# Combination of the experts' rows: two rows of a token sorted by place, the front ones gathered and added during the last expert, no stage of its own

## The chip, the core and the metric

The kernel runs on one core of a Trainium2 chip. The metric is the device time of one launch in microseconds (us), lower is better; the kernel before is shown with the median of three launches. The engines of the core are TensorE (PE in the profile), VectorE (DVE), ScalarE (ACT), GpSimd (POOL) and SyncE (SP, which here only issues transfers), beside 16 DMA engines.

## What is computed

A decoder block over 1,024 tokens of width 1,024: a mixer (linear recurrence and attention side by side), a residual addition, then a mixture of 32 experts, a residual addition and a last RMSNorm. The change is in the last part. Of the reference:

```python
e_in_group = jnp.take_along_axis(e_logits, g_sel[:, :, None], axis=1)[:, 0]
top_v, top_i = lax.top_k(e_in_group, TOP_K)             # TOP_K = 2
comb_w = p_group * jax.nn.softmax(top_v, axis=-1)
expert = g_sel * EXPERTS_PER_GROUP + top_i
...
    hb = jax.nn.silu(xb @ w1[e]) * (xb @ w3[e])
    return hb @ w2[e]
...
out = jnp.zeros((T + 1, D), xn.dtype).at[slot_tok].add(y * slot_w[:, None])[:T]
...
x = x + hierarchical_moe(v, ...)
return rms_norm(x, g_final)
```

Each token goes to two different experts of one group; the output is the residual plus the two experts' rows, each times its weight, and then normed.

## The kernel before

The program is a list of stages (`write`); at the end of each, `stage` clears the semaphores and puts an all-engine barrier. The last two stages are `experts` and `combine`.

**`experts`.** The tokens of an expert fill up to 96 slots (`BLK`); expert j owns the slots 96j to 96j+95 of the DRAM tensor `y_d`. What is over 96 goes to surplus blocks behind slot 96*32; their number n is known only on the chip, and `beyond` runs them under a condition. For each expert, SP loads six 1 MB pieces of weights into a ring of 12 buffers (`e_raw`), ACT makes the high part of each (`piece_hi`), DVE the low part (`piece_lo`, L1505), and PE runs three products for each pair. POOL gathers the tokens of expert j+2 by an indirect transfer (L1575). At the end ACT copies the 96 result rows out of PSUM (`rows_out`, L1649) and issues their store to `y_d` (`rows_store`, L1653), which signals `y_stored[j % 2]`. The experts go through `body(j, b)`, with the copy and the store of expert j-1 inside the pass of expert j. Each engine has its own instruction order, written out by hand; between the first passes DVE also works out the slots of the tokens in small steps (`surplus`, `places`, `destinations`, `blocks`), the slot of a token's first and second choice going to `dest`.

**`combine`.** After the barrier, with eight tiles of 128 tokens: POOL gathers for tile t the two rows of each token from `y_d` (two indirect transfers of 512 KB, L1913) into a ring of four pairs of buffers; DVE adds both, each times its weight, to the residual `x2` (L1956, one operation SCALAR_TENSOR_TENSOR of 128x1024 a row); ACT squares and sums (L1935); DVE makes the mean (L1942); POOL takes its power -0.5 (L1908, `root`); DVE scales by it and by `g_final` (L1949, `norm`); SP stores the tile (L1927). DVE's order is: both additions of t, mean of t-1, norm of t-2.

## Time and profile before

| | |
|---|---|
| three launches | 1899.32, 1899.99, 1902.91 us (median 1899.99) |
| profiled execution | 1900.84 us, span from first to last instruction 1899.2 us |
| busy: PE, DVE, ACT, POOL | 91%, 56%, 45%, 7% of the span |
| matmul share after 1852 us (`combine`) | none |

A row of a timeline is: start in us, duration in us, engine, line of the kernel, operation, output<-input, shapes, count, and in brackets how long the engine had been idle and what ended that. "ACTq" and "SPq" are transfers issued by these engines. A transfer issued by POOL (DMA_INDIRECT) shows the time in which POOL made it ready, not its landing. A row of windows is: the stretch, its length, busy time of each engine with the number of instructions, granted TensorE clock, busy share of the DMA engines, GB/s.

### The profile page before, as it was taken

How to read it: one execution, taken by the hardware profiler on the slowest of the kernel's cores; microseconds unless marked ns; L12 is line 12 of the kernel's file. 1: busy time of each engine (PE TensorE's matmuls, PEld its weight loads, DVE VectorE, ACT ScalarE, POOL GpSimd, SP SyncE). 2: the span in 40 equal slices, each digit the busy share in tenths (PEclk: the TensorE clock that was granted, in tenths of full speed). 3: DMA queues.
4: the chain of work that ended last, by engine and by line, in shares of the span. 5: the costliest groups of instructions: out<-in, count | busy, mean ns of one | idle time of the engine just before them, and what ended most of it. 6: DMA issues, size and time to landing. Idle time of an engine off the chain costs nothing. (4 is left out here: it accounts for less than half of the span.)

```text
span 1899.2 us, 22922 instructions
## 1 busy us (share of the span) xinstructions
PE 1727.1 (91%) x8515; PEld 1375.4 (72%) x8515; DVE 1061.3 (56%) x1211; ACT 849.1 (45%) x861; POOL 131.1 (7%) x179
## 2 busy tenths in 40 slices
PE   4999999999999998988887989959999999999970
PEld 3788888888986887866675879846677777777750
DVE  4343434341215103257775342669988888888856
ACT  5233424241211212135554020237777777777751
POOL 1200000000000000011110000010000000000005
PEclk9999999999999999989998989979999999999995
DMA  5722312223431233534434250179999999999947
GB/s 173 210 89 72 115 66 99 88 88 109 146 122 45 90 113 122 196 133 178 177 121 155 89 181 12 66 251 398 393 399 395 394 400 392 393 397 397 397 193 276
DMA packets 147070, 386.02 MB, mean 203 GB/s; under 512 B 11448, under 2 KB 70920, under 8 KB 142928
## 3 DMA queue, kind: packets, MB, share of 16 engines
q1 hardware_dynamic: 133760, 338.97, 48.0%
q0 software_dynamic: 8384, 29.63, 5.3%
q10 hardware_dynamic: 4880, 16.82, 2.2%
q8 instruction: 28, 0.46, 0.1%
q14 instruction: 18, 0.15, 0.0%
HBM read 317.96 MB, written 67.42 MB: 203 GB/s over the span
## 5 line engine op out<-in xcount | busy, mean ns | idle before, releaser
L1505 DVE TENSOR_TENSOR e_l<-e_raw,e_h 128x2048 fp32r<-128x2048 f32 x192 | 439.4, 2291 | 67.1 <-ACT e_h L1499 66.9
L1499 ACT ACTIVATE e_h<-e_raw 128x2048 fp32r<-128x2048 f32 x192 | 368.0, 1918 | 84.8 <-PE ps L1534 50.1
L196 PE MATMUL ps<-uh,w_h 128*128 128x512 f32 x1024 | 318.2, 392 | 21.2 <-DVE ul L838 13.5
L196 PE MATMUL ps<-ul,w_h 128*128 128x512 f32 x1024 | 317.1, 391 | 0.0
L196 PE MATMUL ps<-uh,w_l 128*128 128x512 f32 x1024 | 316.9, 391 | 0.0
L180 DVE TENSOR_TENSOR w_l<-w_raw,w_h 128x2048 fp32r<-128x2048 f32 x38 | 87.1, 2291 | 349.6 <-ACT w_h L176 349.6
L196 PEld LDWEIGHTS ps<-uh,w_h 128*128 128x128 f32 x1024 | 193.1, 189 | 63.1 <-issue 22.3
L196 PEld LDWEIGHTS ps<-ul,w_h 128*128 128x128 f32 x1024 | 193.5, 189 | 40.5
L196 PEld LDWEIGHTS ps<-uh,w_l 128*128 128x128 f32 x1024 | 193.4, 189 | 40.5
L1521 PE MATMUL ps<-e_h,e_xth 128*96 128x512 f32 x512 | 205.1, 401 | 5.8 <-DVE e_l L1505 2.7
L1521 PE MATMUL ps<-e_h,e_xtl 128*96 128x512 f32 x512 | 202.6, 396 | 0.0
L1521 PE MATMUL ps<-e_l,e_xth 128*96 128x512 f32 x512 | 201.8, 394 | 0.0
L176 ACT ACTIVATE w_h<-w_raw 128x2048 fp32r<-128x2048 f32 x38 | 72.7, 1914 | 228.7 <-DMA w_raw<-w_in 104.5
L208 PE MATMUL ps<-w_h,uh 128*128 128x256 f32 x384 | 112.3, 293 | 10.6 <-DVE ul L1341 5.8
L1521 PEld LDWEIGHTS ps<-e_h,e_xth 128*96 128x96 f32 x512 | 83.0, 162 | 45.7 <-issue 7.2
L208 PE MATMUL ps<-w_l,uh 128*128 128x256 f32 x384 | 110.8, 288 | 0.0
L208 PE MATMUL ps<-w_h,ul 128*128 128x256 f32 x384 | 110.7, 288 | 0.0
L1521 PEld LDWEIGHTS ps<-e_h,e_xtl 128*96 128x96 f32 x512 | 83.0, 162 | 36.2
L1521 PEld LDWEIGHTS ps<-e_l,e_xth 128*96 128x96 f32 x512 | 83.3, 163 | 32.0
L208 PEld LDWEIGHTS ps<-w_h,uh 128*128 128x128 f32 x384 | 75.8, 197 | 13.5 <-issue 6.2
L1534 PE MATMUL ps<-e_h,e_hth 128*96 128x512 f32 x256 | 82.2, 402 | 2.1 <-DVE e_htl L1644 2.1
L987 PE MATMUL ps<-at_qk 128*128 128x512 f32 (+3 forms) x288 | 74.5, 392 | 9.5 <-DVE at_small L1077 6.8
(254 smaller groups left out, 2256.5 us busy)
## 6 DMA issues: line engine op xcount, KB each, us to landing
e_raw<-w_exp_gate SPq DMA_DIRECT2D x64, 1024.0 KB, 20.9
e_raw<-w_exp_up SPq DMA_DIRECT2D x64, 1024.0 KB, 20.8
e_raw<-w_exp_down SPq DMA_DIRECT2D x64, 1024.0 KB, 19.8
w_raw<-w_in SPq DMA_DIRECT2D x28, 1024.0 KB, 5.5
qk_d<-qk SPq DMA_DIRECT2D x16, 1024.0 KB, 4.1
at_qk<-qk_d SPq DMA_DIRECT2D x8, 2048.0 KB, 8.7
y_d<-e_y ACTq DMA_DIRECT2D x32, 384.0 KB, 6.4
y_d<-zeros POOLq DMA_DIRECT2D x22, 384.0 KB, 10.8
```

Of the source, the lines that this page charges most:

```text
L176: act.activation(self.w_h[s][:, :, :], self.w_raw[s][:, :, :], ACT.Copy).then_inc(self.w_hi[s], 1)
L180: dve.tensor_tensor(self.w_l[s][:, :, :], self.w_raw[s][:, :, :], self.w_h[s][:, :, :].bitcast(F32), ALU.subtract).then_inc(self.w_lo[s], 1)
L196: mm = pe.matmul(ps[:, h * HALF:(h + 1) * HALF], w[:, k, :], u[:, k, h * HALF:(h + 1) * HALF], start=first, stop=last)
L208: mm = pe.matmul(ps, u[:, k, rows], w[s][:, k, :], start=first, stop=last)
L987: mm = pe.matmul(k_.ps[n % 2][:, at:end], q, qk[c][:, part, at:end], start=first, stop=last)
L1499: act.activation(self.e_h[m % SPLIT][:, :, :], self.e_raw[slot][:, :, :], ACT.Copy).then_inc(self.e_hi[m % SPLIT], 1)
L1505: dve.tensor_tensor(self.e_l[slot][:, :, :], self.e_raw[slot][:, :, :], self.e_h[m % SPLIT][:, :, :].bitcast(F32), ALU.subtract).then_inc( ...
L1521: mm = pe.matmul(ps, x[:, k, :], w[:, k, :], start=first and first_piece, stop=last and last_piece)
L1534: mm = pe.matmul(ps[:, c * HALF:(c + 1) * HALF], x[:, at, :], w[:, 2 * k + c, :], start=first, stop=last)
```

## The change

`combine` and the barrier ahead of it go away. DVE, in two more places between the first experts, sorts the two slots of each token into the lower (`EARLY`) and the higher (`LATER`), and their weights with them (`row_order`, `shares`). When expert 30's rows are stored, POOL gathers all lower rows into eight buffers `near` and DVE adds them after its last work on expert 31. When all rows are stored, POOL gathers the higher rows into eight buffers `far`; then come addition, squares, mean, power, norm and store as before, the norm writing into `far[t]`. The lower row of a token may lie in a surplus block; then a third gather runs (`SURPLUS`), only if n > 0. `near` and `far` lie over the weights' buffers. `g_final` is loaded behind the last weights. The power -0.5 of the tiles comes on POOL behind all eight `LATER` gathers, where it stood between the gathers before. The core of the diff:

```diff
+        tok = self.tok = high.put("rt_tok", [P, NT], I32)
+        self.rows_of = high.put("rows_of", [P, 3, NT], I32)
+        self.share = high.put("share", [P, 3, NT])
+        self.final_at = high.at
...
+        order = Map(nc, self.list_end + 16 * NE, self.high)
+        dst = [order.put(f"ls_dst{s}", [P, NT]) for s in range(2)]
+        swapped, kept, here, one, two, row = (order.put(f"ls_{n}", [P, NT]) for n in ("swapped", "kept", "here", "one", "two", "row"))
+        final = Map(nc, self.final_at, self.high)
+        g_b = final.put("cb_g", [P, D])
+        total, mean, rstd, power = (final.put(f"cb_{n}", [P, NT]) for n in ("total", "mean", "rstd", "power"))
+        upper = Map(nc, self.act_start, self.raw_end)
+        near, far = ([upper.put(f"cb_{n}{t}", [P, D]) for t in range(NT)] for n in ("near", "far"))
+        EARLY, LATER, SURPLUS = range(3)
...
-        def beyond(engine, body):
+        def beyond(engine, body, before=None, after=None):
 
             engine.wait_ge(listed_out, 1)
             n = engine.value_load(k_.blocks[0:1, n_over:n_over + 1], min_val=0, max_val=MAXX)
             with engine.If(0 < n):
+                if before:
+                    before()
                 with engine.Fori(0, MAXX // 2) as i:
                     for b in range(2):
                         with engine.If(2 * i + b < n):
                             body(NE + 2 * i + b, b, 2 * i + b)
+                if after:
+                    after(n)
             return n
...
-                beyond(sp, other)
+                sp.dma_start(g_b[:, :], k_.ins["g_final"].partition_broadcast(P)).then_inc(g_in, 16)
+                beyond(sp, other, before=lambda: sp.wait_ge(near_added, NT))
+                for t in range(NT):
+                    sp.wait_ge(normed, t + 1)
+                    sp.dma_start(k_.out[t * P:(t + 1) * P, :], far[t][:, :]).then_inc(out_stored, 16)
+                sp.wait_ge(out_stored, 16 * NT)
...
+                pool.memset(power[:, :], -0.5).then_inc(const, 1)
+
+                def rows(which, t, to, done):
+                    upto = BLK * (NE - 1) if which == EARLY else SLOTS
+                    pool.indirect_dma_start(out=to[t][:, :], out_offset=None, in_=k_.y_d[0:upto, :],
+                                            in_offset=bass.IndirectOffsetOnAxis(ap=k_.rows_of[:, which, t:t + 1], axis=0))\
+                        .then_inc(done[t], 16)
+
+                def all_stored(n):
+                    pool.wait_ge(y_stored[0], 16 * (NE // 2 + (n + 1) // 2))
+                    pool.wait_ge(y_stored[1], 16 * (NE // 2 + n // 2))
+
+                def surplus_rows(n):
+                    pool.wait_ge(const, 1)
+                    pool.wait_ge(near_added, NT)
+                    all_stored(n)
+                    pool.tensor_tensor(mean[:, :], power[:, :], power[:, :], ALU.mult).then_inc(surplus_ready, 1)
+                    pool.wait_ge(surplus_ready, 1)
+                    for t in range(NT):
+                        rows(SURPLUS, t, near, near_in)
+
+                pool.wait_ge(ordered, 3)
+                pool.wait_ge(y_stored[0], 16 * (NE // 2))
+                pool.wait_ge(y_stored[1], 16 * (NE // 2 - 1))
+                for t in range(NT):
+                    rows(EARLY, t, near, near_in)
+                n = beyond(pool, lambda j, b, t: gather(pool, j, b, None, t), after=surplus_rows)
+
+                all_stored(n)
                 pool.wait_ge(idx_in[0], 16 * (n // 2 + 1))
                 pool.wait_ge(idx_in[1], 16 * ((n + 1) // 2))
+                pool.wait_ge(const, 1)
+                pool.tensor_tensor(rstd[:, :], power[:, :], power[:, :], ALU.mult).then_inc(const, 1)
+                pool.wait_ge(const, 2)
+                for t in range(NT):
+                    rows(LATER, t, far, far_in)
+                for t in range(NT):
+                    pool.wait_ge(averaged, t + 1)
+                    pool.tensor_tensor(rstd[:, t:t + 1], mean[:, t:t + 1], power[:, t:t + 1], ALU.pow).then_inc(powered, 1)
...
+                for t in range(NT):
+                    act.wait_ge(added, t + 1)
+                    act.activation(near[t][:, :], k_.x2[:, t, :], ACT.Square, accum_out=total[:, t:t + 1]).then_inc(squared, 1)
...
+                LAST = BLK * (NE - 1)
+
+                def row_order():
+                    tt(swapped[:, :], dst[0][:, :], dst[1][:, :], ALU.is_gt)
+                    tt(kept[:, :], dst[0][:, :], dst[1][:, :], ALU.is_le)
+                    tt(row[:, :], dst[0][:, :], dst[1][:, :], ALU.max)
+                    dve.tensor_copy(k_.rows_of[:, LATER, :], row[:, :]).then_inc(ordered, 1)
+                    tt(dst[0][:, :], dst[0][:, :], dst[1][:, :], ALU.min)
+                    did(dve.tensor_scalar(here[:, :], dst[0][:, :], float(LAST), None, ALU.is_lt))
+                    did(dve.tensor_scalar(dst[1][:, :], dst[0][:, :], float(LAST - 1), None, ALU.min))
+                    dve.tensor_copy(k_.rows_of[:, EARLY, :], dst[1][:, :]).then_inc(ordered, 1)
+                    did(dve.tensor_scalar(dst[0][:, :], dst[0][:, :], float(LAST), None, ALU.max))
+                    dve.tensor_copy(k_.rows_of[:, SURPLUS, :], dst[0][:, :]).then_inc(ordered, 1)
+
+                def shares():
+                    for which, of_kept, of_swapped in ((LATER, 1, 0), (EARLY, 0, 1)):
+                        tt(one[:, :], kept[:, :], k_.wgt[:, of_kept, :], ALU.mult)
+                        tt(two[:, :], swapped[:, :], k_.wgt[:, of_swapped, :], ALU.mult)
+                        tt(k_.share[:, which, :], one[:, :], two[:, :], ALU.add)
+                    tt(one[:, :], k_.share[:, EARLY, :], here[:, :], ALU.mult)
+                    tt(k_.share[:, SURPLUS, :], k_.share[:, EARLY, :], one[:, :], ALU.subtract)
+                    did(dve.tensor_copy(k_.share[:, EARLY, :], one[:, :]))
+
+                def add(rows, which, t, done):
+                    dve.scalar_tensor_tensor(out=k_.x2[:, t, :], in0=rows[t][:, :], scalar=k_.share[:, which, t:t + 1],
+                                             in1=k_.x2[:, t, :], op0=ALU.mult, op1=ALU.add).then_inc(done, 1)
+
+                def surplus_rows(n):
+                    dve.wait_ge(near_added, NT)
+                    for t in range(NT):
+                        dve.wait_ge(near_in[t], 32)
+                        add(near, SURPLUS, t, surplus_added)
+                    dve.wait_ge(surplus_added, NT)
+
+                def average(t):
+                    dve.wait_ge(squared, t + 1)
+                    dve.tensor_scalar(mean[:, t:t + 1], total[:, t:t + 1], 1.0 / D, EPS, ALU.mult, ALU.add).then_inc(averaged, 1)
+
+                def norm(t):
+                    dve.wait_ge(powered, t + 1)
+                    dve.scalar_tensor_tensor(out=far[t][:, :], in0=k_.x2[:, t, :], scalar=rstd[:, t:t + 1],
+                                             in1=g_b[:, :], op0=ALU.mult, op1=ALU.mult).then_inc(normed, 1)
...
+                body(4, 0)
+                row_order()
+                body(5, 1)
+                shares()
+                in_pairs(dve, body, 3, NE // 2 - 1)
                 body(NE - 2, 0, True)
                 j, b = NE - 1, 1
                 k_.piece_lo(dve, (j, b, 4))
                 hidden(dve, j, (j, b, 3))
                 k_.piece_lo(dve, (j, b, 5))
                 h_low(dve, j)
+                for t in range(NT):
+                    dve.wait_ge(near_in[t], 16)
+                    add(near, EARLY, t, near_added)
...
-                beyond(dve, other)
-
-    def combine(self):
...
+                beyond(dve, other, after=surplus_rows)
                 dve.wait_ge(g_in, 16)
                 for t in range(NT):
...
+                    dve.wait_ge(near_added, t + 1)
+                    dve.wait_ge(far_in[t], 16)
+                    add(far, LATER, t, added)
                     if t >= 1:
-                        averages(t - 1)
+                        average(t - 1)
                     if t >= 2:
                         norm(t - 2)
-                averages(NT - 1)
+                average(NT - 1)
                 for t in (NT - 2, NT - 1):
                     norm(t)
...
-                             (self.experts,), (self.combine,)):
+                             (self.experts,)):
```

How the instructions stand on the engines, at three places. POOL at the end, before: `cb_y` are the buffers of the ring, one row a gather.

```order
L1579 DMA e_idx_5175<-slots_d 96x1
L1664 TENSOR_LOAD blocks
...
L1903 MEMSET cb_power 128x8
L1913 DMA cb_y_8525<-y_d,dest 128x1024
L1913 DMA cb_y_8526<-y_d,dest 128x1024
...
L1913 DMA cb_y_8532<-y_d,dest 128x1024
L1908 TENSOR_TENSOR cb_rstd<-cb_mean,cb_power 128x1
```

And in the changed kernel: `near` for the lower rows, `far` for the higher.

```order
L1593 DMA e_idx_5175<-slots_d 96x1
L1738 MEMSET cb_power 128x8
L1742 DMA cb_near_6655<-y_d,rows_of 128x1024
...
L1742 DMA cb_near_6662<-y_d,rows_of 128x1024
L1678 TENSOR_LOAD blocks
...
L1770 TENSOR_TENSOR cb_rstd<-cb_power 128x8
L1742 DMA cb_far_6663<-y_d,rows_of 128x1024
...
L1742 DMA cb_far_6670<-y_d,rows_of 128x1024
L1776 TENSOR_TENSOR cb_rstd<-cb_mean,cb_power 128x1 x8
```

Eight of the sixteen gathers now stand ahead of the read of n, and all powers stand behind the last gather.

DVE between expert 4 and the next weights, in the changed kernel; before, row L1505 stood right behind the row of `e_xtl`.

```order
L1637 TENSOR_TENSOR e_xtl_6632<-ps,e_xth_6630 128x768
L1870 TENSOR_TENSOR ls_swapped<-ls_dst_6642,ls_dst_6643 128x8
L1870 TENSOR_TENSOR ls_kept<-ls_dst_6642,ls_dst_6643 128x8
L1870 TENSOR_TENSOR ls_row<-ls_dst_6642,ls_dst_6643 128x8
L1908 CAST rows_of<-ls_row 128x8
L1870 TENSOR_TENSOR ls_dst_6642<-ls_dst_6642,ls_dst_6643 128x8
L1910 TENSOR_SCALAR ls_here<-ls_dst_6642 128x8
L1911 TENSOR_SCALAR ls_dst_6643<-ls_dst_6642 128x8
L1912 CAST rows_of<-ls_dst_6643 128x8
L1913 TENSOR_SCALAR ls_dst_6642<-ls_dst_6642 128x8
L1914 CAST rows_of<-ls_dst_6642 128x8
L1508 TENSOR_TENSOR e_l_5165<-e_raw_5153,e_h_5169 128x2048
```

Ten small operations are new there, and nine more of the same size stand behind expert 5 (`shares`).

DVE in the combination, before (from its second tile):

```order
L1956 SCALAR_TENSOR_TENSOR x_5167<-cb_y_8527,wgt,x_5167 128x1024
L1956 SCALAR_TENSOR_TENSOR x_5167<-cb_y_8528,wgt,x_5167 128x1024
L1942 TENSOR_SCALAR cb_mean<-cb_total 128x1
L1956 SCALAR_TENSOR_TENSOR x_5167<-cb_y_8529,wgt,x_5167 128x1024
L1956 SCALAR_TENSOR_TENSOR x_5167<-cb_y_8530,wgt,x_5167 128x1024
L1942 TENSOR_SCALAR cb_mean<-cb_total 128x1
L1949 SCALAR_TENSOR_TENSOR cb_o_8533<-x_5167,cb_rstd,cb_g 128x1024
```

and in the changed kernel:

```order
L1926 SCALAR_TENSOR_TENSOR x_5167<-cb_far_6664,share,x_5167 128x1024
L1938 TENSOR_SCALAR cb_mean<-cb_total 128x1
L1926 SCALAR_TENSOR_TENSOR x_5167<-cb_far_6665,share,x_5167 128x1024
L1938 TENSOR_SCALAR cb_mean<-cb_total 128x1
L1942 SCALAR_TENSOR_TENSOR cb_far_6663<-x_5167,cb_rstd,cb_g 128x1024
L1926 SCALAR_TENSOR_TENSOR x_5167<-cb_far_6666,share,x_5167 128x1024
```

One large addition a tile has gone from here to a place ahead of it; the norm of the first tile stands behind three additions and ahead of five.

## Rows read from the trace of the kernel before

**Rows 1.** The page: its first line, and one of its transfers.

```profile
span 1899.2 us, 22922 instructions
...
y_d<-e_y ACTq DMA_DIRECT2D x32, 384.0 KB, 6.4
```

**Rows 2.** Windows: middle experts, last products, gap, combination.

```profile
1400.00:1800.00 400.00, 400.00 (x1902) 282.78 (x1901) 352.54 (x204) 316.43 (x228) 31.73 (x23) 1.00 1.03 396
1838.00:1845.00 7.00, 6.98 (x24) 4.42 (x22) 0.00 (x0) 0.00 (x0) 0.00 (x0) 0.76 0.02 5
1845.00:1852.00 7.00, 0.00 (x0) 0.00 (x0) 0.00 (x0) 1.02 (x1) 0.00 (x0) 0.75 0.19 57
1852.00:1899.00 47.00, 0.00 (x0) 0.00 (x0) 30.33 (x32) 9.21 (x16) 27.12 (x25) 0.50 0.77 279
```

**Rows 3.** Timeline of POOL, combination.

```profile
1853.48 1.00 POOL L1913 DMA_INDIRECT cb_y<-y_d,dest  x1 [0.65 <-POOL cb_power L1903]
1854.79 0.95 POOL L1913 DMA_INDIRECT cb_y<-y_d,dest  x1 [0.31 <-issue]
...
1861.29 1.72 POOL L1913 DMA_INDIRECT cb_y<-y_d,dest  x1 [0.30 <-issue]
1863.32 0.97 POOL L1913 DMA_INDIRECT cb_y<-y_d,dest  x1 [0.30 <-issue]
1864.96 1.53 POOL L1908 TENSOR_TENSOR cb_rstd<-cb_mean,cb_power 128x1 f32<-128x1 f32 x1 [0.67 <-DVE cb_mean L1942]
...
1869.52 0.74 POOL L1908 TENSOR_TENSOR cb_rstd<-cb_mean,cb_power 128x1 f32<-128x1 f32 x1
```

**Rows 4.** Timeline of DVE, last expert and combination.

```profile
1837.02 0.55 DVE L1644 TENSOR_TENSOR e_htl<-ps,e_hth 128x384 fp32r<-128x384 f32 x1
1858.89 1.28 DVE L1956 SCALAR_TENSOR_TENSOR x<-cb_y,wgt,x 128x1024 f32<-128x1024 f32 x1 [21.32 <-DMA cb_y<-y_d,dest]
...
1864.79 2.60 DVE L1956 SCALAR_TENSOR_TENSOR x<-cb_y,wgt,x 128x1024 f32<-128x1024 f32 x2
...
1868.56 2.60 DVE L1956 SCALAR_TENSOR_TENSOR x<-cb_y,wgt,x 128x1024 f32<-128x1024 f32 x2
...
1892.08 1.28 DVE L1949 SCALAR_TENSOR_TENSOR cb_o<-x,cb_rstd,cb_g 128x1024 f32<-128x1024 f32 x1 [0.27 <-POOL cb_rstd L1908]
1894.37 1.28 DVE L1949 SCALAR_TENSOR_TENSOR cb_o<-x,cb_rstd,cb_g 128x1024 f32<-128x1024 f32 x1 [1.01 <-DMA out<-cb_o]
```

**Rows 5.** Timeline of ACT: stores of experts 30 and 31 issued.

```profile
1831.51 0.33 ACTq L1653 DMA_DIRECT2D y_d<-e_y  x1
...
1846.07 0.32 ACTq L1653 DMA_DIRECT2D y_d<-e_y  x1
```

**Rows 6.** Tile `e_y` over the whole run: its 32 stores.

```profile
DMA to landing us min/median/max: 3.0/6.4/6.8
```

**Rows 7.** Transfers from 1846 to 1850 us: line, KB, us to landing.

```profile
y_d<-e_y ACTq DMA_DIRECT2D x1, 384.0 KB, 3.0
```

**Rows 8.** Timeline of DVE, experts 2 to 5.

```profile
1334.44 0.17 DVE L1834 CAST dest<-ls_dst 128x8 int32<-128x8 f32 x1
1334.65 0.43 DVE L1812 TENSOR_TENSOR rt_oh<-rt_oh,rt_ebase 128x256 f32<-128x256 f32 x1
...
1351.29 0.95 DVE L1623 TENSOR_TENSOR e_xtl<-ps,e_xth 128x768 fp32r<-128x768 f32 x1
1352.16 0.87 DVE L1812 TENSOR_TENSOR ls_before<-ls_ends,ls_jj 1x704 f32<-1x704 f32 x1
...
1354.58 4.49 DVE L1505 TENSOR_TENSOR e_l<-e_raw,e_h 128x2048 fp32r<-128x2048 f32 x2
...
1370.11 0.95 DVE L1623 TENSOR_TENSOR e_xtl<-ps,e_xth 128x768 fp32r<-128x768 f32 x1
...
1387.81 0.95 DVE L1623 TENSOR_TENSOR e_xtl<-ps,e_xth 128x768 fp32r<-128x768 f32 x1
```

**Rows 9.** Line L1209: the same power on POOL, DVE mostly idle.

```profile
L1209 POOL TENSOR_TENSOR rt_rstd<-rt_mean,rt_power x8: 549/550/573, 1182.5 to 1241.3; 128x1 f32<-128x1 f32 x8
```

More of the change, by code:

```diff
@@ L1134, in project_route @@
             put(f"rt_{n}", [P, NT]) for n in ("gmax", "m1", "m2", "gsum", "ex", "inv", "sel", "dst"))
-        tok = self.tok = put("rt_tok", [P, NT], I32)
         lists = Map(nc, mix_at + 3 * PIECE, self.work_start)
@@ L1141, in project_route @@
         self.list_end = high.at
-        assert high.at + 16 * NE + 4 * NT <= self.high
+        assert high.at + 16 * NE + 4 * 8 * NT <= self.high
         self.before = Map(nc, lists.at, self.work_start).put("ls_before", [1, NX, NE])
@@ L1551, in experts @@
                                    for n, name in enumerate(("cnt", "extra", "ends", "shift")))
-        dst = Map(nc, self.list_end + 16 * NE, self.high).put("ls_dst", [P, NT])
+        order = Map(nc, self.list_end + 16 * NE, self.high)
[7 more added lines that the diff above has]
+        EARLY, LATER, SURPLUS = range(3)
         sem = self.sem
@@ L1556, in experts @@
             sem("e_" + n) for n in ("x_mm", "x_hi", "x_lo", "silu", "hid", "h_mm", "h_hi", "h_lo", "y_out"))
-        list_own, dest_out, listed_out, scattered = (sem("ls_" + n) for n in ("own", "dest", "listed", "scattered"))
+        list_own, dest_out, listed_out, scattered, ordered = (sem("ls_" + n) for n in ("own", "dest", "listed", "scattered", "ordered"))
+        near_in, far_in = ([sem(f"cb_{n}_in{t}") for t in range(NT)] for n in ("near", "far"))
+        g_in, const, surplus_ready, near_added, surplus_added, added, squared, averaged, powered, normed, out_stored = (
+            sem("cb_" + n) for n in ("g", "const", "surplus_ready", "near_added", "surplus", "added", "squared", "averaged", "powered", "normed", "stored"))
         by_chunk = lambda ps: ps.rearrange("p (k t) -> p k t", t=P)[:, :, 0:BLK]
@@ L1832, in destinations @@
                         tt(k_.oh[s][:, :, :], k_.oh[s][:, :, :], e_base, ALU.mult)
-                        did(dve.tensor_reduce(dst[:, :], k_.oh[s][:, :, :], AX.X, ALU.add))
-                        dve.tensor_copy(k_.dest[:, s, :], dst[:, :]).then_inc(dest_out, 1)
+                        did(dve.tensor_reduce(dst[s][:, :], k_.oh[s][:, :, :], AX.X, ALU.add))
+                        dve.tensor_copy(k_.dest[:, s, :], dst[s][:, :]).then_inc(dest_out, 1)
                         dve.wait_ge(dest_out, s + 1)
@@ L1951, in _ @@
+                beyond(dve, other, after=surplus_rows)
                 dve.wait_ge(g_in, 16)
                 for t in range(NT):
-                    x2 = k_.x2[:, t, :]
-                    for s in range(2):
-                        dve.wait_ge(got[t % RING][s], 16 * (t // RING + 1))
-                        dve.scalar_tensor_tensor(out=x2, in0=yg[t % RING][s][:, :], scalar=k_.wgt[:, s, t:t + 1], in1=x2,
-                                                 op0=ALU.mult, op1=ALU.add).then_inc((first, added)[s], 1)
-                        if s == 0:
-                            dve.wait_ge(first, t + 1)
+                    dve.wait_ge(near_added, t + 1)
+                    dve.wait_ge(far_in[t], 16)
+                    add(far, LATER, t, added)
```

62 lines of the change are left out of this document (removed).

## The prediction

> **What bounds the kernel now.** I read the windows first. In the middle of the experts' stage PE is busy in all of the stretch at clock 1.00 while the transfer engines stand at a share of 1.03 and 396 GB/s; then the last expert's down products run with the transfer engines at 0.02, seven us follow in which only one ACT copy is busy, and the combination takes 47 us without a matmul, DVE busy for 30.3 of them and the transfer engines at 0.77 [rows 2]. So there are three things at the end: idle transfer engines under PE's last work, a gap, and a stage of DVE's and POOL's own. The timelines date them. Expert 31's store is issued at 1846.07 [rows 5] and lands 3.0 us later, at 1849.1 [rows 7]; POOL's first gather starts only at 1853.48 [rows 3]: 4.4 us from landing to gather, mostly the barrier. The first addition starts at 1858.89, 5.4 us behind its gather, and the last norm ends at 1894.37 + 1.28 = 1895.65 [rows 4]; the span ends at 1899.2 [rows 1], 3.55 us later, the last store. I call the start of the first gather that needs all rows T0. Before it is 1853.48, and the end is T0 + 45.7.
>
> In between, a tile costs DVE 1868.56 - 1864.79 = 3.77 us [rows 4] for two additions, a norm and a mean: three large operations at 1.24 us and 0.06 for the mean. 24 of them are 29.8 us; the rest of the 45.7 are first arrival, end and waits.
>
> **What moves ahead of T0.** There were 32 stores to `y_d`, so n = 0 [rows 1] and no surplus runs. Two experts of a token are never the same, so the lower row is always of expert 30 or before, and the first eight gathers hold every token's lower row. They wait for expert 30's store: issued at 1831.51 [rows 5], landed about 3.0 later as the equal store of expert 31 [rows 7], 1834.5. POOL has nothing else then. DVE's last work ends at 1837.6 [rows 4], so eight additions (8 x 1.24 = 9.9 us) can follow the arrivals. Eight gathers took POOL from 1853.48 to 1863.32 + 0.97 = 1864.29, 10.8 us [rows 3], and with 5.4 us from the last one's start to its row the last lower row is there about 15.3 us after the first gather's start, some 1851, added by 1852.5. The higher rows can't be there before T0 + 5.4, so the additions are hidden with some 5 us to spare; without that cover they cost up to 9.9.
>
> **What it adds.** 19 small DVE operations between experts 4 and 6. An operation of 128x8 takes 0.17 and the next starts 0.21 after it [rows 8], so 10 x 0.21 = 2.1 us and 9 x 0.21 = 1.9. What such an insert costs is seen at the last of the four in the kernel before: five operations from 1352.16 to 1354.58, 2.42 us, stand in a pass of 1370.11 - 1351.29 = 18.82 us, the pass behind it takes 17.70 [rows 8]; so 1.12 us of the 2.42 lengthen the pass and 1.30 are slack. By the same slack the new ones cost 0.8 + 0.6 = **+1.4 us**. Bounds: nothing, and the whole 4.0. PE waits for these low parts, and as it has no idle time in the passes behind, the loss isn't caught up. Everything below is 1.4 later: the last store is issued at 1847.5.
>
> **Its landing.** 3.0 us when alone [rows 7], 6.4 as median beside weights at 396 GB/s, at most 6.8 [rows 6]. Beside it the tail of the front gathers' 4.2 MB is still moving, but nearly over. I take 3.3, near the lone end: 1850.8. The Trainium skill ("DMA: Bandwidth & Descriptors", § Queues, rings and completion order) says that each DMA engine goes round between the queues that have work, so that the store wouldn't stand behind all of the gathers. That no row of this kernel isolates; with a backlog of 8 gathers first in line it would be the rival of the late store below.
>
> **From landing to T0.** The barrier is replaced by a few waits, a small POOL operation and the wait on it. The nearest POOL operation is the power at 0.55 [rows 9], and from a small operation's end to a gather 0.65 passed [rows 3]; with a little for the wait 1.25 (bounds 0.75 and 1.6). **T0 = 1852.0**, 1.4 us earlier than before: the barrier gives 3.1, the inserts take 1.4 and the landing 0.3. The read of n on POOL's queue hides while the front gathers are made ready.
>
> **From T0 to the end.** DVE's order is addition 0, 1, 2, then norm 0. Norm 0 needs POOL's power 0, and that now stands behind all eight gathers: POOL is free at T0 + 10.8 as above, then 0.2 and a power of 0.74 (uncontended; 1.53 beside DVE work [rows 3]), so norm 0 starts at T0 + 11.9. The three additions end near T0 + 10, so DVE idles about 2 us, and additions 3 to 7 queue behind it, their rows already there. Behind norm 0 stand in all 8 norms and 5 additions: 13 x 1.24 + 5 x 0.06 = 16.4, T0 + 28.3. The 0.3 us before the last but one norm [rows 4] stays; the 1.01 before the last norm, a wait for one of two output buffers, goes. T0 + 28.6, and the store's 3.55: **T0 + 32.15**, against T0 + 45.7. The stores (4.2 MB) and the gathers (4.2 MB) in that time are 8.4 MB in 31 us, under the 279 GB/s that the stage showed. Bounds: eight gathers without DVE beside them 7 x 1.25 + 0.95 = 9.7, all at 1.72 + 0.30 16.2 [rows 3]; so -1.1 and +5.4.
>
> **Sum.** 1852.0 + 32.15 = 1884.15, against a span of 1899.2: -15.05. The profiled execution (1900.84) is 0.85 above the median; taken off the median of 1899.99 it gives **1885 us**. All low bounds together (-1.4 - 0.3 - 0.5 - 1.1) give 1881.7; the high ones wouldn't come together, +2.6 + 3.5 + 0.35 + 5.4 + 0.8 = +12.7.
>
> **Rivals.**
> - *Late store.* The store of expert 31 waits behind the front gathers, and these run at the 279 GB/s of the combination [rows 2] instead of quickly: 4.2 MB / 279 = 15 us from 1837.5, 1852.5, then the store's 1.4 and landing, T0 about 1856: 1889. For: store 31 is issued when some gathers are still out. Against: the quiet transfer engines.
> - *POOL starved.* Beside DVE's additions gathers took 1.72 instead of 0.95, the power 1.53 instead of 0.74 [rows 3]. If each front gather waits out a whole addition, eight take 9.7 + 8 x 1.28 = 20 us, T0 is 1857, and the far ones, with three additions beside them, are up to 2.7 longer: about 1893. The delay that the rows show, 1.72 - 0.95 = 0.77, is less than a whole addition. The Trainium skill ("SBUF — State Buffer", § Who interferes with whom) has such a rule, a DVE instruction with two SBUF inputs and a GpSimd one that reads SBUF exclude each other for a whole instruction. By that rule, the longer 1.72 and 1.53 agree in sign, and whether the wait is for the whole addition they don't show.
> - *Less is lost.* Inserts hidden, DVE doesn't wait for power 0, store at 3.0: 1879 to 1881.
> - *It doesn't do what it says.* The front gathers wait for something that comes late (the order's signal, n's read) and only the barrier is saved: 1896 to 1900.
> - *Slower.* With DMA at a share of 1.03 [rows 2] there is no reserve: if the late DVE work throws the weights' ring out of step, each later pass is longer. 26 passes follow, so it is slower from 0.58 us a pass; at 0.8, as one insert costs, 20.8 - 15 = +6, 1906. Against: after the insert of [rows 8] the pass is at once 17.70 again.
>
> **How the numbers follow.** Forecast (1881.7 to 1888) 0.66, late store 0.14, starved 0.06, less lost 0.08, not as said 0.03, slower 0.03. The range that leaves out under 2 in 10 goes from 1880.5 to 1891; the likeliest case's own is 1881.7 to 1888. 0.2% (3.8 us) is about what a measurement can tell from no change: faster 0.95, same 0.02, slower 0.03.
>
> **What would show it.** `near` gathers start at about 1836, additions to `x2` from 1841 beside the down products; the passes with the inserts 18.5 and 18.3 us and 17.7 behind; first `far` gather about 1852; DVE idle before norm 0 for about 2 us, put down to POOL, then 2.5 us a tile with no wait; the last norm at T0 + 28.6. Wrong would be a `far` gather after 1856, a wait for arrivals in DVE's later tiles, or passes over 17.8 us from expert 7 on.

## The result, and the profile after

The changed kernel takes **1888.21 us** (median of eight launches, 1883.18 to 1894.58), the kernel before, on the same chip in turn with it, 1902.72 us (1896.51 to 1905.67): ratio 0.9935, 95% interval 0.9917 to 0.9952, so by the ratio 12.4 us (9 to 16) less, and 14.5 between the two medians. The prediction was a difference of 15 us and 1885 us, range 1880.5 to 1891.

Its profiled execution took 1891.58 us with a span of 1890.1, 9.1 us under the span of [rows 1]. A part of the difference between single executions lies ahead of the experts' stage, where the change touches nothing: in this pair the changed kernel enters the stage about 5 us later. So I read times inside the stage, from marks that every kernel has: **A** is the start of the third `e_xtl` row on DVE, at 1295.99 before and at 1301.12 in the changed kernel; **S** is the issue of expert 31's store; **T0**, as in the prediction, is the first gather that needs all rows. For the kernel before, these are A + 550.08, A + 557.49 and the end at A + 603.21 (S from [rows 5], T0 from [rows 3], the end from [rows 1]).

The page, the two stores and the second one's landing, which answer to [rows 1], [rows 5] and [rows 7]:

```profile
span 1890.1 us, 22892 instructions
...
1837.46 0.33 ACTq L1667 DMA_DIRECT2D y_d<-e_y  x1
...
1851.73 0.32 ACTq L1667 DMA_DIRECT2D y_d<-e_y  x1
...
y_d<-e_y ACTq DMA_DIRECT2D x1, 384.0 KB, 5.8
```

S is A + 550.61. The store takes 5.8 us where the equal one before took 3.0, and this is the largest thing that the prediction didn't have. The packets of the transfer queues tell how: q10 carries the store, q0 the gathers. From the issue at 1851.73 to 1854.13 none of the store's packets moves; then come these, up to its landing:

```profile
q0 software_dynamic: 228, 0.83, 69.7%
q10 hardware_dynamic: 112, 0.39, 28.7%
```

In e1 below, with no gather beside it, the store's first packets move between 0.8 and 1.2 us behind the issue, here between 2.4 and 2.8: it first waits 1.6 us longer, and then goes among the gathers' packets, not behind all of them. POOL's timeline from the first gather of the lower rows (`near`) to the powers, which answers to [rows 3]:

```profile
1841.25 2.67 POOL L1742 DMA_INDIRECT cb_near<-y_d,rows_of  x1 [59.25 <-DMA y_d<-e_y]
1844.22 0.95 POOL L1742 DMA_INDIRECT cb_near<-y_d,rows_of  x1 [0.30 <-issue]
...
1853.35 1.76 POOL L1742 DMA_INDIRECT cb_near<-y_d,rows_of  x1 [0.30 <-issue]
1857.89 0.59 POOL L1770 TENSOR_TENSOR cb_rstd<-cb_power 128x8 f32<-128x8 f32 x1 [2.78 <-DMA y_d<-e_y]
1858.75 0.95 POOL L1742 DMA_INDIRECT cb_far<-y_d,rows_of  x1 [0.27 <-POOL cb_rstd L1770]
...
1868.22 0.95 POOL L1742 DMA_INDIRECT cb_far<-y_d,rows_of  x1 [0.31 <-issue]
1869.18 1.11 POOL L1776 TENSOR_TENSOR cb_rstd<-cb_mean,cb_power 128x1 f32<-128x1 f32 x2
```

POOL is free at 1855.11 and waits 2.78 us for the store; the bracket names what it waits for. T0 is 1858.75, A + 557.63: **no earlier than before**. The whole gain is behind T0, on DVE (answers to [rows 4]):

```profile
1847.25 1.28 DVE L1926 SCALAR_TENSOR_TENSOR x<-cb_near,share,x 128x1024 f32<-128x1024 f32 x1 [3.74 <-DMA cb_near<-y_d,rows_of]
...
1860.33 2.54 DVE L1926 SCALAR_TENSOR_TENSOR x<-cb_near,share,x 128x1024 f32<-128x1024 f32 x2 [1.91 <-DMA cb_near<-y_d,rows_of]
1863.05 1.28 DVE L1926 SCALAR_TENSOR_TENSOR x<-cb_far,share,x 128x1024 f32<-128x1024 f32 x1 [0.18 <-DMA cb_far<-y_d,rows_of]
1865.81 1.28 DVE L1926 SCALAR_TENSOR_TENSOR x<-cb_far,share,x 128x1024 f32<-128x1024 f32 x1 [1.48 <-DMA cb_far<-y_d,rows_of]
...
1869.80 1.28 DVE L1942 SCALAR_TENSOR_TENSOR cb_far<-x,cb_rstd,cb_g 128x1024 f32<-128x1024 f32 x1 [1.33 <-POOL cb_rstd L1776]
```

Two things are to be seen. The last two lower rows are added from 1860.33 to 1862.87, and DVE has 0.18 us before the first higher row: the cover that hides the eight lower additions is used up. And behind norm 0 DVE waits only once, 0.33 us for POOL ahead of the last two norms; a tile takes 2.46 us, and the last norm ends at T0 + 27.52, the span at T0 + 31.35 (T0 + 45.7 before). From A to the end it is 588.98 us against 603.21, **14.2 less**. The last stretch in one row of windows, beside the last of [rows 2]: DVE now has 18 large operations in it, the last two lower additions among them, where it had 24.

```profile
1858.70:1890.00 31.30, 0.00 (x0) 0.00 (x0) 22.62 (x26) 9.20 (x16) 17.50 (x16) 0.50 0.72 272
```

### The profile page after: what moved, and what is told of

Its sections match the earlier page's. It is cut to its first block and busy times, and to the rows that moved or that the text cites. A ratio compares the mean times of both kernels' runs of the same rounds, so it can differ in the third digit from the quotient of the medians.

```text
span 1890.1 us, 22892 instructions
## 1 busy us (share of the span) xinstructions
PE 1731.3 (92%) x8515; PEld 1378.1 (73%) x8515; DVE 1063.5 (56%) x1230; ACT 848.3 (45%) x861; POOL 133.5 (7%) x180
## 6 DMA issues: line engine op xcount, KB each, us to landing
y_d<-zeros POOLq DMA_DIRECT2D x22, 384.0 KB, 10.9
```

## The experiments

Eleven runs. The theory that I brought to them: the store lands late because the gathers of the lower rows are moving beside it; the inserts cost what the slack of a pass doesn't take; norm 0 waits for a power that stands behind eight gathers. Each has a rival below. Where only one execution was looked at, the comparison goes by A, S and T0. The changed kernel profiled a second time (e11) has 589.90 from A to the end where the first time had 588.98, so a difference under 1 us in that sum is none.

**e1_hold_front: no barrier, and no overlap either.** The gathers of the lower rows wait for the last store too, so nothing is overlapped, but there is still no barrier.

```diff
-                pool.wait_ge(y_stored[1], 16 * (NE // 2 - 1))
+                pool.wait_ge(y_stored[1], 16 * (NE // 2))
```

> One edit to the changed kernel: the gathers of the lower rows wait for expert 31's store as well, so nothing is in the transfer engines when that store is issued. S is the issue of that store; in the changed kernel it lands at S + 5.84 and the span ends at S + 38.4; before, at S + 3.0 and S + 53.1. Traffic theory (the front gathers' data delay the store): lands at S + 3.0 to 3.5. Rival (the store is slow for another reason, such as its place in the new stage): still about S + 5.8. The end: all 16 gathers and 24 large operations of DVE behind S, so S + 43 to S + 46, that is 5 to 8 us above the changed kernel and 7 to 10 below the one before; this is what the missing barrier and the unlocked buffers are worth without the overlap. If the overlap were worth nothing, S + 38.

The store, and the first gather behind it:

```profile
1848.14 0.32 ACTq L1667 DMA_DIRECT2D y_d<-e_y  x1
...
1851.97 1.00 POOL L1742 DMA_INDIRECT cb_near<-y_d,rows_of  x1 [73.61 <-DMA y_d<-e_y]
...
y_d<-e_y ACTq DMA_DIRECT2D x1, 384.0 KB, 3.0
```

With no gather beside it the store lands in 3.0 again. The median is 1897.72 us, ratio to before 0.998 (0.9963 to 0.9997); A to the end is 599.89. So taking the barrier away, with the inserts that the change needs still in, is worth 603.21 - 599.89 = 3.3 us (3.8 by the launches' ratio, 0.6 to 7.0), and the overlap 599.89 - 588.98 = 10.9. The end, S + 49.26, missed my 43 to 46: I had the higher rows follow quickly, but the eight gathers of the lower rows, with DVE's additions beside them, take 12.6 us from the first one's start, and the first of the higher rows starts only at S + 16.47.

**e4_spread_small and e7_spread_all: the inserts.** The new small operations stood in two blocks, behind experts 4 and 5. In e4 the same operations stand in five blocks behind experts 4 to 8, at most six to a pass; in e7 DVE's small operations of the whole stage, the older ones too, are spread over experts 0 to 13. The core of e4:

```diff
+                row_order2()
+                body(6, 0)
+                share_of(LATER, 1, 0)
+                body(7, 1)
+                share_of(EARLY, 0, 1)
+                body(8, 0)
                 shares()
-                in_pairs(dve, body, 3, NE // 2 - 1)
+                body(9, 1)
+                in_pairs(dve, body, 5, NE // 2 - 1)
```

> The 19 small DVE operations stand in six groups of at most six behind experts 4 to 8 (four to six each, 0.8 to 1.2 us) instead of ten and nine behind 4 and 5. Slack theory (a pass takes 1.3 us of extra DVE work for nothing): all passes behind expert 5 take 17.7 us and the sum from the first pass to expert 31's store is 1.0 us less than in the changed kernel (549.6 instead of 550.6 from the low part of expert 2's rows to that store's issue). Rival (each small operation costs as much wherever it stands): the same 1.0 us, spread over five passes.

> All small DVE work of the experts' stage, old and new, in 14 groups of at most 1.3 us, one behind each of experts 0 to 13. Slack theory: every pass takes 17.7 us, so the sum from expert 2's low part to expert 31's store falls from 550.6 (549.7 with only the new work spread) to 546.4: 4.2 us less than the changed kernel. Rival: groups near 1.3 us (two operations of 0.87) still lengthen a pass by 0.1 to 0.4, 547.5.

The start of the same DVE row (`e_xtl`) once a pass, first in the changed kernel, where two passes have inserts:

```profile
1375.10 0.95 DVE L1637 TENSOR_TENSOR e_xtl<-ps,e_xth 128x768 fp32r<-128x768 f32 x1
...
1393.12 0.95 DVE L1637 TENSOR_TENSOR e_xtl<-ps,e_xth 128x768 fp32r<-128x768 f32 x1
...
1411.52 0.95 DVE L1637 TENSOR_TENSOR e_xtl<-ps,e_xth 128x768 fp32r<-128x768 f32 x1
...
1429.20 0.95 DVE L1637 TENSOR_TENSOR e_xtl<-ps,e_xth 128x768 fp32r<-128x768 f32 x1
```

These are passes of 18.02, 18.40 and 17.68 us. In e4 they are gone:

```profile
1373.32 0.95 DVE L1637 TENSOR_TENSOR e_xtl<-ps,e_xth 128x768 fp32r<-128x768 f32 x1
...
1390.99 0.95 DVE L1637 TENSOR_TENSOR e_xtl<-ps,e_xth 128x768 fp32r<-128x768 f32 x1
...
1408.64 0.95 DVE L1637 TENSOR_TENSOR e_xtl<-ps,e_xth 128x768 fp32r<-128x768 f32 x1
```

17.67 and 17.65. A to S is 549.71 against 550.61, and A to the end 587.78. What the passes give is seen better from A to DVE's last low part for the products (`e_htl` of expert 31), as the products behind it differ by themselves: 541.85 in the changed kernel (541.79 to 541.92 in all eight other runs with the same inserts), 540.67 in e4. So 1.18 comes back, all of the 1.06 us that the two long passes have over 17.68. The slack theory holds.

In e7 A to S is 547.16, 3.45 us less than in the changed kernel and near the expectation of 546.4, but not for the reason expected. From A to the last low part it is 539.72, only 2.13 less. The other 1.32 are expert 31's last products, from that low part to S, first in the changed kernel, then in e7:

```profile
1842.97:1851.73 8.76, 7.08 (x24) 4.60 (x24) 3.89 (x5) 1.02 (x1) 6.93 (x7) 0.81 0.78 264
```

```profile
1831.37:1838.81 7.44, 5.76 (x24) 3.79 (x24) 2.76 (x4) 1.02 (x1) 5.92 (x6) 1.00 0.68 230
```

The same 24 products run at a granted clock of 0.81 on average in the one (0.5 at its start, 1.00 at its end) and at 1.00 throughout in the other. In the 2.00 us ahead PE was busy for 0.48 in both. In every other run but e10 this stretch takes 8.74 to 9.05 us at 0.81. Why the clock stayed up in e7 and e10 is open; these two share the spread inserts. At the end e7 has nothing of the 1.32: A to the end is 586.85, again 2.13 less.

The passes give 2.13 and not the 4.2 expected because only the early ones are shorter. They are 17.6 to 17.7, the late ones 17.8 to 18.0:

```profile
1771.42 0.95 DVE L1637 TENSOR_TENSOR e_xtl<-ps,e_xth 128x768 fp32r<-128x768 f32 x1
...
1789.40 0.95 DVE L1637 TENSOR_TENSOR e_xtl<-ps,e_xth 128x768 fp32r<-128x768 f32 x1
```

The waits from 1400 to 1820 us say why. A row is: who waits, for what, us in all, how often, the longest in us. First the changed kernel, then e7:

```profile
ACT e_h L1502 <- DMA e_raw<-w_exp_up: 2.0, 3, 0.8
ACT e_h L1502 <- DMA e_raw<-w_exp_down: 1.5, 2, 0.9
```

```profile
ACT e_h L1502 <- DMA e_raw<-w_exp_down: 23.1, 24, 1.6
ACT e_h L1502 <- DMA e_raw<-w_exp_up: 15.5, 24, 0.7
```

When no pass is held up, the passes outrun the weights, and the transfers set the pace: 48 waits for weights against 5. Six pieces of 128x2048, a gather and a store of 96x1024 are 7.1 MB a pass, at the 397 GB/s of e7's late passes 17.8 us; the changed kernel moves 395 GB/s there, so the rate itself can't tell the two apart, and the waits do. That the slow early passes of the changed kernel let the ring fill, which its later passes then live on, is argued from its five waits. That also answers the "slower" rival of the prediction from the other side: the transfers have next to no reserve, but a long pass gives them time and takes none.

**e2_front_from_29, e5_hold_adds, e6_psum_input: gathers beside additions.** In e2 the lower rows are those in the blocks up to expert 29, so that the gathers start an expert earlier and are to be through before S. It leaves out the lower row of a token whose two experts are 30 and 31. The gathers also wait until PE has used the four pieces of weights that lie under their buffers (`piece_done`).

```diff
-                    upto = BLK * (NE - 1) if which == EARLY else SLOTS
+                    upto = BLK * (NE - 2) if which == EARLY else SLOTS
...
-                pool.wait_ge(y_stored[0], 16 * (NE // 2))
+                pool.wait_ge(y_stored[0], 16 * (NE // 2 - 1))
                 pool.wait_ge(y_stored[1], 16 * (NE // 2 - 1))
+                for m in (6, 7, 8, 9):
+                    k_.piece_done(pool, (NE - 3, 1, m))
...
-                LAST = BLK * (NE - 1)
+                LAST = BLK * (NE - 2)
```

e5 is e2 with one more line, which holds the additions back until all eight rows are there, and e6 is e2 with the second tensor of the addition read from PSUM instead of the residual (which it leaves out), so that it has only one input in SBUF:

```diff
+                for t in range(NT):
                     dve.wait_ge(near_in[t], 16)
```

```diff
-                    add(near, EARLY, t, near_added)
+                    dve.scalar_tensor_tensor(out=k_.x2[:, t, :], in0=near[t][:, :], scalar=k_.share[:, EARLY, t:t + 1],
+                                             in1=k_.ps[0][:, :], op0=ALU.mult, op1=ALU.add).then_inc(near_added, 1)
```

> The gathers of the lower rows start when expert 29's rows are stored (one pass earlier), once the weights' buffers under them are used up; the threshold is expert 30's first slot. Left out: the lower row of a token whose two experts are 30 and 31 (it isn't added). All else stands. Traffic theory: the front rows are there before expert 31's store is issued, which lands at S + 3.0 to 3.5 instead of S + 5.84; the eight additions follow each other from the end of DVE's work on expert 31 without a wait (9.9 us) and end 3 us ahead of the first higher row; the end is S + 35.6, 2.8 below the changed kernel. Rival (the store is slow by its place): S + 5.8 and S + 38. Second rival: the 4.2 MB beside the last weights delay these, and the passes of experts 30 and 31 grow by up to 5 us, so that S comes later from the first pass and nothing is gained.

> As the kernel with the front gathers one pass earlier (it leaves out the lower row of tokens with both experts in 30 and 31), where the seventh of these gathers took POOL 10.29 us while DVE ran six additions without a gap. Here DVE first waits for all eight front rows and adds then. Lock theory (additions with both inputs in the on-chip buffers keep POOL from making a gather ready, as long as they follow each other without a gap): the seventh and eighth gather take 0.9 to 2.7 us, all front rows are there by S - 1 (S: issue of expert 31's store), that store lands at S + 3.0 to 3.5, and the higher rows' first gathers meet the eight additions and are slow in their turn. Rival (the seventh gather waited for room in the queue behind the weights or for its data path): it takes about 10 us again.

> As the kernel with the front gathers one pass earlier, and the eight front additions read PSUM instead of the residual (left out: the residual, so the output is not the block's; DVE's time for an operation of 128x1024 stays about 1.2 to 1.3 us). DVE is as busy as there, but with one input in the on-chip buffers instead of two. Lock theory in the form 'two inputs': the seventh gather takes 1 to 2.7 us instead of 10.29. Rival 'any busy DVE': about 10 us again. With the gathers free: front rows all there before S, store at S + 3.0 to 3.5, T0 at S + 4.2 to 4.7.

In e2 the passes aren't longer (A to S 550.71), yet the store lands in 5.1, with the rows of the last two gathers beside it, and the gain over the changed kernel is small: 1887.44 us, ratio to before 0.9939 (0.9917 to 0.9961), A to the end 588.49. POOL and DVE show what came between:

```profile
1829.65 10.29 POOL L1742 DMA_INDIRECT cb_near<-y_d,rows_of  x1 [0.30 <-issue]
1831.88 7.25 DVE L1928 SCALAR_TENSOR_TENSOR x<-cb_near,share,x 128x1024 f32<-128x1024 f32 x6
1840.25 0.94 POOL L1742 DMA_INDIRECT cb_near<-y_d,rows_of  x1 [0.30 <-issue]
...
y_d<-e_y ACTq DMA_DIRECT2D x1, 384.0 KB, 5.1
```

One gather takes 10.29 us while DVE runs six additions back to back, and ends 0.8 us behind the last of them; the next one, with DVE idle, takes 0.94. In e5, with no additions beside it, the same gather takes 2.65 us, and the store lands in 3.0. The 2.65 are themselves a gather beside a low part, DVE's work on weights, whose two inputs lie in SBUF too: it ends at 1839.00, again 0.8 behind the low part's end (1835.91 + 2.28).

```profile
1835.91 2.28 DVE L1508 TENSOR_TENSOR e_l<-e_raw,e_h 128x2048 fp32r<-128x2048 f32 x1
1836.35 2.65 POOL L1742 DMA_INDIRECT cb_near<-y_d,rows_of  x1 [0.30 <-issue]
...
y_d<-e_y ACTq DMA_DIRECT2D x1, 384.0 KB, 3.0
...
1844.59 9.66 DVE L1928 SCALAR_TENSOR_TENSOR x<-cb_near,share,x 128x1024 f32<-128x1024 f32 x8 [5.93 <-DMA cb_near<-y_d,rows_of]
...
1851.03 1.66 POOL L1742 DMA_INDIRECT cb_far<-y_d,rows_of  x1 [0.32 <-POOL cb_rstd L1772]
1852.99 2.08 POOL L1742 DMA_INDIRECT cb_far<-y_d,rows_of  x1 [0.30 <-issue]
```

What the store gains, the far gathers lose: the additions now lie beside them (1.66 and 2.08 instead of 0.95), norm 0 waits 2.63, and the end is S + 37.78 as in e2. These rows also bound what e2 says. The eight additions start 1.20 us apart, as closely as e2's six, and the gather that starts at 1851.03 beside the sixth (1850.58 to 1851.86) ends at 1852.69, 0.8 behind that one's end and in the middle of the next. So a gather isn't always held until the last of a row of additions; why the one in e2 was, this record doesn't show. The clean answer on what holds it is e6:

```profile
1841.81 2.65 POOL L1742 DMA_INDIRECT cb_near<-y_d,rows_of  x1 [0.30 <-issue]
1844.04 9.61 DVE L1983 SCALAR_TENSOR_TENSOR x<-cb_near,share,ps 128x1024 f32<-128x1024 f32 x8
1844.77 0.94 POOL L1742 DMA_INDIRECT cb_near<-y_d,rows_of  x1 [0.30 <-issue]
```

The additions start 0.42 us before this gather would end, just as in e2, run back to back as in e2, and cost the gathers nothing. So neither DVE's being busy nor the transfers beside it hold a gather up; the second input in SBUF does. A to the end is 586.25, end S + 35.38.

The Trainium skill ("SBUF — State Buffer", § Who interferes with whom) says that a DVE instruction with two SBUF inputs and a GpSimd instruction that reads SBUF exclude each other for a whole instruction. By that rule, the trace agrees that it is these operations, and e5's gathers end 0.8 us behind the end of one of them; e2 shows more than the page says, a gather held past one 1.28 us instruction, through six of them.

**e3_power_between, e8_power_two: where the first powers stand.** POOL's power 0 stands behind all eight gathers. e3 puts it behind the sixth, e8 puts powers 0 and 1 behind the sixth and seventh.

```diff
                 for t in range(NT):
                     rows(LATER, t, far, far_in)
+                    if t == 5:
+                        root(0)
```

> The power of tile 0 stands behind the sixth gather of the higher rows instead of behind the eighth. Theory: DVE's wait of 1.33 us ahead of norm 0 goes (0 to 0.3 left), and with it 1.0 to 1.3 us from T0 (first gather of higher rows) to the last norm's end, 27.5 to about 26.3; the two gathers behind the power start up to 1.5 later, and their rows are needed only 8 us after that. Rival: the gathers' data, not the power, bound DVE, so the wait moves to additions 3 to 7 and the 27.5 stays.

> The powers of tiles 0 and 1 stand behind the sixth and the seventh gather of the higher rows (with only the first moved, norm 0 waited 0.35 but norm 1 waited 1.48, and T0 to the last norm's end was 28.8 instead of 27.5). Theory (POOL's order decides): both norms wait under 0.4 and T0 to the last norm's end is 26.3 to 26.8. Rival (POOL is slowed by the additions and norms that now start earlier, so what the power gains the gathers lose): the last two gathers take 1.5 to 2 us each and the sum stays 27.5 to 28.8.

DVE's norm 0 and norm 1 in e3:

```profile
1864.74 1.28 DVE L1946 SCALAR_TENSOR_TENSOR cb_far<-x,cb_rstd,cb_g 128x1024 f32<-128x1024 f32 x1 [0.35 <-POOL cb_rstd L1774]
...
1868.76 1.28 DVE L1946 SCALAR_TENSOR_TENSOR cb_far<-x,cb_rstd,cb_g 128x1024 f32<-128x1024 f32 x1 [1.48 <-POOL cb_rstd L1774]
```

The wait moves from norm 0 (1.33) to norm 1 (1.48). In e8 the three first norms wait 0.35, 0.40 and 0.39, together nearly the 1.33 that norm 0 waited, and the last two gathers take 1.99 and 2.00 beside the additions. T0 to the last norm's end is 28.77 (e3) and 28.13 (e8) against 27.52; A to the end 591.11 and 590.38 against 588.98. Not all of that is the power's place: in both, the first gather of the higher rows takes 1.70 and 1.75 where it took 0.95, because three lower additions lie beside it. From the first higher addition to the last norm's end it is 23.69 (e3) and 23.03 (e8) against 23.22, and 23.07 in e11. The rival holds: an earlier power gains nothing.

**e9_two_groups, e10_best, e11_changed_again: a better version.** Two experts of one token lie in the same group. e9 gives the last two places to experts of different groups (30 changes places with 22, a group's width before), so that every token's lower row is in a block ahead of the last two; then e2's early start leaves nothing out. DVE starts to add only when all eight gathers are made ready, which keeps the additions off them:

```diff
+OTHER = NE - 2 - EG
+def at_place(j):
+    return {OTHER: NE - 2, NE - 2: OTHER}.get(j, j) if type(j) is int else j
...
                     rows(EARLY, t, near, near_in)
+                pool.memset(total[:, :], 0.0).then_inc(made, 1)
...
                 h_low(dve, j)
+                dve.wait_ge(made, 1)
```

e10 is e9 with the spread of e7, e11 the changed kernel once more beside it, on the same chip.

> The early front gathers made whole: the places of experts 22 and 30 in the order are swapped (weights, slots, lists of tokens), so the last two experts are of different groups, no token has both, and every lower row is stored once expert 29's place is. DVE starts its front additions only when POOL has made all eight gathers ready (a POOL memset behind them signals it), so that the additions don't keep POOL out. Theory (traffic and lock together): the seventh gather takes under 2.8 us, additions from about S - 6.7 to S + 3.3, store lands at S + 3.0 to 3.5, T0 at S + 4.0, end at S + 35.4, 3 us less than the changed kernel's S + 38.4. Rival: the additions' end after S + 3 still meets the higher rows' first gathers (T0 to last norm's end 29 instead of 27.5), end S + 37. From expert 2's low part to S 550.7 as before, if the unrolled order of SP costs nothing.

> Early front gathers with the swapped places and the gate for DVE's additions, and all small DVE work in 14 groups of at most 1.3 us. From expert 2's low part to S 547.2 as with the groups alone (550.6 in the changed kernel) and S + 35.4 behind it: 582.6 against 589.0, so 6 us below the changed kernel and 20 below the one before (ratio 0.9895). Rival: late passes that are already at 17.9 us with the groups alone are bound by the weights' transfers, and 4.2 MB of front rows beside the last weights come on top; then 3 to 4 us of it are lost again (585 to 586).

> The changed kernel unchanged, on the same chip as the combined version, for the comparison of the two: ratio to the kernel before 0.992 to 0.995 as measured. Its intervals show how much one execution differs from another: the store of expert 31 lands at S + 5.4 to 6.1, the end at S + 38 to 40.

POOL and DVE in e9:

```profile
1833.06 2.65 POOL L1754 DMA_INDIRECT cb_near<-y_d,rows_of  x1 [0.30 <-issue]
...
1836.94 0.13 POOL L1778 MEMSET cb_total<- 128x8 f32 x1
1837.11 9.66 DVE L1941 SCALAR_TENSOR_TENSOR x<-cb_near,share,x 128x1024 f32<-128x1024 f32 x8 [1.74 <-POOL cb_total L1778]
...
1847.87 0.96 POOL L1754 DMA_INDIRECT cb_far<-y_d,rows_of  x1 [0.50 <-POOL cb_rstd L1785]
...
1854.83 1.89 POOL L1754 DMA_INDIRECT cb_far<-y_d,rows_of  x1 [0.30 <-issue]
...
1860.18 1.28 DVE L1957 SCALAR_TENSOR_TENSOR cb_far<-x,cb_rstd,cb_g 128x1024 f32<-128x1024 f32 x1 [2.63 <-POOL cb_rstd L1791]
```

All eight additions are made by S + 2.91, the store lands in 3.0 and T0 is S + 4.01, where it was S + 7.02. The end is S + 36.64, 1.2 over the 35.4 expected and near the rival's 37: gathers of the higher rows are slower beside additions (1.89), and norm 0 waits 2.63. A to the end is 587.51. e10 comes to 584.39, between the 582.6 expected and the rival's 585 to 586. Its A to S is 547.18, and as in e7 that isn't the passes alone: A to the last low part is 539.70, 2.13 under e9 by the spread, and the last products take 7.48 at a granted clock of 1.00 where e9 has 9.04 at 0.81. So 2.1 of the 3.1 us that it is ahead of e9 at the end are the spread's; whether the 1.0 left is this clock or the scatter of single executions isn't shown. Its end is S + 37.21; its store took 3.8, which I can't place. Six launches give **1880.68 us** (1876.95 to 1886.47), ratio to before 0.9891 (0.9869 to 0.9913): it beats both kernels. The changed kernel beside it has 1887.40, ratio 0.9933 (0.9909 to 0.9958), with a landing of 6.2, A to the end 589.90. The two intervals just touch, but five of e10's six launches lie under all six of the changed kernel's.

## Why the prediction was right, step by step

The mechanism and the sign were right, and the time is 3.2 us over the forecast: in the range, and 0.2 over the 1888 at which the likeliest case's own range ended. One term was too small (+2.5 us) and three things came out 1.7 smaller than said; that they nearly cancel is luck.

- *Inserts, +1.4.* The two long passes have 0.34 + 0.72 = 1.06 over 17.68; from A to the last low part it is 541.85 where it was 541.03, so +0.82, and e4 gives 1.18 back. Passes of 17.7 behind them, as said. Right in kind, and 0.2 to 0.6 too much. A to S grew by 0.53 only, because the last products took 8.76 us instead of 9.05, both at a granted clock of 0.81; the sum had no term for that.
- *Landing of the last store, 3.3.* **This term was mis-sized: 5.84** (5.4 to 6.2 in all executions with the changed kernel's early gathers beside it, 3.0 where none is, e1). I took the tail of the gathers for nearly over, at about 1851 for the last row. But the first gather started only 3.8 us behind the issue of store 30 and then took 2.67 beside a low part of two SBUF inputs, and four later ones took 1.32 to 1.77; the last is made ready at 1855.11, 3.4 us after S. This is the "late store" rival in a milder form: delayed by 2.8 us, not by all the traffic that was ahead. By the rule of the Trainium skill that the prediction named ("DMA: Bandwidth & Descriptors", § Queues, rings and completion order), each DMA engine goes round between the queues that have work. The trace agrees for the store's packets once they move (112 among 228 of the gathers'), and shows 1.6 us of delay ahead of the first of them; what holds that one up isn't shown.
- *Landing to T0, 1.25.* 1.18.
- *T0, 1.4 us earlier.* 0.1 later: -1.5 as worked out, + 2.5 for the landing, - 0.9 for inserts and last products.
- *The lower rows, hidden with 5 us to spare.* Hidden, but with 0.18. The seventh of these rows is on DVE only at S + 8.60, and the last one, 8.2 us after its gather's start, lands at 1861.55: 20.3 us after the first gather instead of 15.3. So the landing and the late lower rows don't add up: by these rows, a store that lands in 3.0 would have brought the higher rows 2.8 us sooner to a DVE that was still adding lower ones until 1862.87, and gained next to nothing. That is argued; what was run is e5, where the store is cured and the additions are late (end S + 37.78 against 38.37), and e6, where both are cured (S + 35.38).
- *Norm 0 at T0 + 11.9, DVE idle for 2.* T0 + 11.05, and 1.48 + 1.33 of waits in two places. The terms that the prediction names add up to 11.74, not 11.9; the power took 0.55 and not 0.74, as two of them take 1.11. How long norm 0 waits depends on how far POOL is when the third higher addition ends. Here POOL is in its last gather, made ready at 1869.17, 0.8 behind that addition's end at 1868.36. Where norm 0 waits 2.63 (e1, e5, e7, e9, e10), it is the last but one gather that ends 0.8 behind, and the last one needs 1.25 more.
- *The tail, T0 + 32.15.* T0 + 31.35, 2.46 a tile. The eight gathers took 10.4 us (10.8 said), the end behind the last norm 3.8 (3.55 said).
- *The sum, -15.05 in the span.* From A: -14.2, in e11 -13.3; launches -12.4 by the ratio, -14.5 by the medians. From the barrier, inserts paid, come 3.3 (3.1 less 1.4 said for T0), from the overlap 10.9 (e1).
- *The rival "POOL starved".* It wasn't the case here: no lower gather but the first took over 1.77 us. In the changed kernel the rows come one by one and leave DVE gaps (waits of 0.34 to 1.9 us between additions); that the gathers get through in these is argued. Its mechanism is real, though, and on one gather stronger than I priced it: 7.6 us in e2, where DVE had no gap.

Open: why one gather in e2 was held through six additions and one in e5 through one; why the clock stayed at 1.00 under the last products of e7 and e10, and whether it does in other launches of them. No power on another engine was tried, nor a last store cut in two.

## What to carry to other kernels

When work is moved under an earlier stage, ask for what it does to the last transfer of that stage and to the engine that makes its transfers ready: the overlap gave 10.9 us, while that store came 2.8 us later and the early rows only just in time. Keep DVE operations with two SBUF inputs off GpSimd's gathers, by one wait for the last gather made ready, or, where the values allow it, by an input from PSUM (e6 shows only the time of that); rows that arrive early are worth nothing if their additions hold up the next gather. And where a stage looks bound by one engine, look how much the next limit leaves: here 0.2 us a pass lay between the pace of the matmuls and that of the weights. And before a shorter stretch is put down to an edit, look at the granted clock in it: 1.3 of e7's 3.45 us were that, and nothing of it is seen at the end.

## What the runs showed of the hardware

- A gather on POOL (128 rows of 4 KB) takes 0.95 us alone and took 10.29 beside six back-to-back SCALAR_TENSOR_TENSOR with two SBUF inputs (e2), 1.66 beside others as close (e5), and 0.94 beside eight with one input from PSUM (e6).
- A store of 384 KB lands in 3.0 us alone, in 3.8 in e10, in 5.1 with the rows of two gathers beside it (e2), in 5.4 to 6.2 beside the last of eight (changed kernel, e3, e4, e7, e8, e11).
- The store's first packets move 0.8 to 1.2 us behind its issue when it is alone (e1, e5, e9), 2.4 to 2.8 beside gathers (changed kernel, e2).
- Without held-up passes the weights' transfers set 17.9 us a pass; held to the matmuls' pace it is 17.7 (e7).
- Expert 31's last products, from the last low part to the issue of the store, take 7.44 and 7.48 us at a granted clock of 1.00 (e7, e10) and 8.74 to 9.05 at 0.81 (all others).
